# State-space stage of a three-layer model: outputs in four quarter arrays and two PSUM banks, taps in the angles' bank, skip term on TensorE, low parts on GpSimd

## The chip, the cores and the metric

The kernel runs on one core of one Trainium2 chip. The metric is device time in microseconds (us) of one execution; lower is better. The kernel before takes 1944.32 us, the median of three runs (1943.21, 1944.32, 1945.85).

## What is computed

Three layers on 512 tokens of width 1024, in float32: a state-space (S5) mixer with a gated output projection and a feed-forward block, an attention layer with selected keys and its feed-forward block, and a hybrid layer with its feed-forward block. The change lies in the first mixer alone. Cut to that:

```python
def s5_mixer(u, lam_re, lam_im, log_dt, b_re, b_im, c_re, c_im, d_skip, w_glu):
    lam = lax.complex(lam_re.astype(f32), lam_im.astype(f32))
    dt = jnp.exp(log_dt.astype(f32))[:, None]
    a_bar = jnp.exp(lam * dt)                               # 64 groups x 64 states
    b_bar = ((a_bar - 1.0) / lam)[..., None] * lax.complex(b_re.astype(f32), b_im.astype(f32))
    bu = jnp.einsum('blgh,gph->blgp', ug, b_bar)            # 16 channels in a group
    _, states = lax.associative_scan(_ssm_combine, (a_seq, bu), axis=1)
    y = jnp.einsum('blgp,ghp->blgh', states, c).real.reshape(bsz, length, D_MODEL)
    y = y + d_skip.astype(f32) * u.astype(f32)
    y = jax.nn.gelu(y).astype(u.dtype)
    val, gate = jnp.split(y @ w_glu, 2, axis=-1)
    return val * jax.nn.sigmoid(gate)
```

## The kernel before

The program is written for each engine apart, with semaphores between the engines; each engine runs its own list in order. After the S5 stage come eleven phases of weight streaming ("glu", "gu0", "down0" and so on), each a long row of matrix products on TensorE (PE). Their weights come in units of 128 x 1024 numbers: SyncE (SP) issues the load of a unit, ScalarE (ACT) writes its high part (`split_hi`, L221), GpSimd (POOL) its low part (`split_lo`, L228), and PE multiplies three times (L238 to L240). Such products start when the low parts of the first two units are there.

The S5 stage works on 8 groups of channels at a time, in 8 steps e = 0 to 7: `begin` (step 0), `step` (1 to 6) and `finish` (7), each engine having its own version. The sequence is cut into 64 chunks of 8 tokens. Buffers that end in `[p]` exist twice, for even and odd steps.

- VectorE (DVE), `matrices(e)` L652: rounds the angles (L659, from PSUM), builds the input matrices `winT` from two tables and two copies of B (L665, L670, L675: 128 x 1024, both inputs in SBUF), and clamps the exact angles (L678). `recurrence(e)` L691: rotates, scans (L711) and rotates back the chunk states, L703 to L721, the sources in PSUM. `tables(e)` L723 adds the skip term `dI` to the taps `conv` (L726). `low(e)` L684 writes the low part of a finished output row (L688). A middle step is `matrices(e + 1)`, `recurrence(e)`, `tables(e + 1)`, `low(e - 1)`.
- PE, middle step: `angle_parts(e + 1)` (L842 to L844), `turn_outputs(e - 1)` (L854, 32 records), `matrices(e + 1)`: four transposes (L771), the taps (L779, 8 products in 16 records of 128 x 32), four transposes (L771); then `outputs(e)`: the products with the taps' shifted table `toep` (L810), `inputs(e + 1)` (L794), `angle_sums(e + 2)` (L836), and the 32 products of states and output tables (L820, 64 records: each float32 product is two records). `outputs` writes one PSUM bank, Y_BANK. The groups 0 to 3 have their states in partitions 0 to 63 and write there, the groups 4 to 7 use partitions 64 to 127, and the order `SIDES` alternates between the two.
- ACT, middle step: `gelu(e - 1)` (table load, L493, high part L496), `matrices_out(e + 1)` (`win` L504 twice, taps L509), `angles(e + 1)` (table load, L473 to L478), `outputs(e)` (L516, the outputs out of PSUM), the decays (L481) and the inputs (L488).
- POOL, middle step: `weigh(e + 2)` (L408), `inputs(e + 1)` (L384), `states_out(e)`: the four output tables (L392, 128 x 512 each), after a wait for the outputs of step e - 2.
- SP: eight DMAs in a step (L338) shift the taps into `toep`; when those of step 7 have been issued, it waits for the last matrices, output tables and decays, whose buffers the weights take over, and issues the first loads of "glu" (L201).

The waits that the order hangs on, in SP's `shift_taps` and in DVE's `tables`:

```python
                sp.wait_ge(S["conv_ready"], e + 1)
                sp.wait_ge(S["y_done"], e + 1)
```

```python
                dve.wait_ge(S["conv_copied"], e + 2)
                dve.tensor_tensor(conv[0:GH, :, :], conv[0:GH, :, :], dI[0:GH, bass.ds(e * QG, QG), :], ALU.add)
                dve.drain().then_inc(S["conv_ready"], 1)
```

Of the kernel before, what the change touches and what calls it, by code (L numbers as in the profile page):

```python
# [14 lines left out]
P = 128  # L15
D = 1024
# [109 lines left out]
def build(nc, d, out):  # L126

    ctx = ExitStack()
    with ctx:
# [148 lines left out]
        def s5two(name, shape):  # L278
# [31 lines left out]
            "wout_ready", "winT_ready", "psT_ready", "psT_free", "convps", "conv_copied", "conv_ready", "w_ready",  # L310
# [42 lines left out]
        PT_BANK, ANG_BANK, CONV_BANK, Z_BANK, Y_BANK, YT_BANK = (0, 4), 1, 2, (3, 6), 5, 7  # L353
# [7 lines left out]
        round_ps, exact_ps = (ps[:, ANG_BANK, n * QP * NC:(n + 1) * QP * NC] for n in range(2))  # L361
        b_raw = [braw[:, n, :].rearrange("p (g h) -> p g h", h=GH) for n in range(2)]

        def s5_gpsimd(pool):
# [31 lines left out]
            def skips():  # L396

                pool.wait_ge(S["par_landed"], 16)
                pool.wait_ge(S["cx_landed"], 16 * 3)
                pool.tensor_tensor(dskip[0:GH, :], dskip[0:GH, :], gain5[0:GH, :], ALU.mult)  # L400
                pool.drain()
                pool.tensor_tensor(dI[0:GH, :, :], bc(dskip[0:GH, :], 2, GH), bc(ident[0:GH, 0:GH], 1, G), ALU.mult)
# [31 lines left out]
        def s5_scalar(act):  # L434
# [63 lines left out]
            def matrices_out(e, p, use):  # L498
# [8 lines left out]
                if not (isinstance(before, int) and before == 0):  # L507
                    act.wait_ge(toep_landed[1 - p], before * (16 * CH))
                act.activation(conv[:].rearrange("p (q g) h -> p q g h", q=2),  # L509
                               ps[:, CONV_BANK, 0:QG * GH].rearrange("p (g q h) -> p q g h", g=QP, q=2), ACT.Copy)\  # L510
                    .then_inc(S["conv_copied"], 1)

            def outputs(e):
                act.wait_ge(S["yT_ready"], e + 1)
                act.wait_ge(S["y_done"], e + 3)
                act.activation(y_q[:].rearrange("p t (g h) -> p g t h", g=4),  # L516
                               ps[:, Y_BANK, :].rearrange("p (g t h) -> p g t h", g=4, t=CH), ACT.Copy)\
                    .then_inc(S["y_evac"], 1)

            def begin(e, p, use):  # L520
# [5 lines left out]
                act.activation(t8T[0:2 * QP, 4:6, :], ps[0:2 * QP, Y_BANK, 0:2 * P].rearrange("p (e n) -> p e n", n=P), ACT.Copy)\  # L526
# [22 lines left out]
        def s5_vector(dve):  # L549
# [102 lines left out]
            def matrices(e, p):  # L652
# [5 lines left out]
                if on_pe:  # L658
                    dve.tensor_scalar(whole[:], round_ps, ROUND, -ROUND, ALU.add, ALU.add).then_inc(S["ang_rounded"], 1)  # L659
                else:  # L660
                    dve.tensor_scalar(turns, ang_sum[:], ROUND, -ROUND, ALU.add, ALU.add)
# [14 lines left out]
                if on_pe:  # L676
                    dve.wait_ge(S["ang_exact"], e)
                    dve.tensor_scalar(ang[:].rearrange("p g c -> p (g c)"), exact_ps, 0.5, -0.5, ALU.min, ALU.max)\  # L678
# [4 lines left out]

            def low(e, p):  # L684

                dve.wait_ge(S["yhi_ready"], e + 1)
                at_ = bass.ds(e, 1)
                dve.tensor_tensor(h_lo[:, at_, :], t32[p][:].unsqueeze(1), h_hi[:, at_, :].bitcast(F32), ALU.subtract)\  # L688
                    .then_inc(S["ylo_ready"], 1)
# [33 lines left out]
            def tables(e, p):  # L723

                dve.wait_ge(S["conv_copied"], e + 2)
                dve.tensor_tensor(conv[0:GH, :, :], conv[0:GH, :, :], dI[0:GH, bass.ds(e * QG, QG), :], ALU.add)  # L726
                dve.drain().then_inc(S["conv_ready"], 1)

            def begin(e, p, use):
# [4 lines left out]
                tables(e, p)  # L734
# [3 lines left out]
                tables(e + 1, 1 - p)  # L738

            def step(e, p, use):  # L740
                matrices(e + 1, 1 - p)
                recurrence(e, p)
                tables(e + 1, 1 - p)
# [10 lines left out]
        def s5_tensor(pe):  # L754
# [10 lines left out]
            def matrices(e):  # L765
# [9 lines left out]
                turned(0)  # L775
                pe.wait_ge(S["conv_copied"], e + 1)
                for g in range(QP):
                    for r in range(2):
                        conv_last = pe.matmul(ps[:, CONV_BANK, 2 * g * GH:2 * (g + 1) * GH],  # L779
                                              winT[:, QP * r + g, :, :].rearrange("p t h -> p (t h)"),  # L780
                                              c_pair[:, bass.ds(e * QP + (GP * r + g), 1), :].rearrange("p a h -> p (a h)"),
                                              start=r == 0, stop=r == 1)
# [16 lines left out]
            SIDES = [g + 4 * half for g in range(4) for half in range(2)]  # L799

            def outputs(e, p, use, between=None):
# [4 lines left out]
                def out_of(g):  # L806
                    return ps[half_of(g), Y_BANK, (g % 4) * P:(g % 4 + 1) * P]

                for g in SIDES:
                    pe.matmul(out_of(g), u_q[p][:, g, :], toep[p][:, :, g, :], start=g % 4 == 0, stop=False)  # L810
# [5 lines left out]
                for r in range(2):  # L816
                    for table in (wout[p], wout_im[p]):
                        for g in SIDES:
                            rows, v = half_of(g), QP * r + g % QP
                            last = pe.matmul(out_of(g), zout[p][rows, v, :], table[rows, v, :, :], start=False,  # L820
                                             stop=r == 1 and table is wout_im[p] and g % 4 == 3)
                last.then_inc(S["y_done"], 1)

            def transposed_ratio():

                pe.wait_ge(S["turn"], 3)
                for e in range(2, NQ):
                    bank = YT_BANK if e < 6 else Y_BANK
# [4 lines left out]
            def angle_sums(e):  # L833

                pe.wait_ge(S["ang_reduced"], e)
                pe.matmul(round_ps, t8T[0:2 * QP, e - 2, :], chunks[0:2 * QP, 0, :], start=True, stop=True)\  # L836
                    .then_inc(S["ang_ready"], 1)

            def angle_parts(e):

                pe.wait_ge(S["ang_rounded"], e - 1)
                pe.matmul(exact_ps, ident, whole[:], start=True, stop=False)  # L842
                pe.matmul(exact_ps, t8T[0:2 * QP, e - 2, :], chunks[0:2 * QP, 1, :], start=False, stop=False)
                pe.matmul(exact_ps, t8T[0:2 * QP, e - 2, :], chunks[0:2 * QP, 2, :], start=False, stop=True)\  # L844
# [1851 lines left out]
```

## Time and profile before

| | |
|---|---|
| median of three runs | 1944.32 us |
| the profiled execution, its own time | 1944.47 us |
| its span in the profile | 1942.4 us |
| of it, the S5 stage up to the first weight product | 133.56 us |
| PE busy in the span | 1890.6 us (97%) |
| DVE, ACT, POOL busy in the span | 774.6, 807.5, 856.8 us |

The profile's times count from the start of the span. "Busy" of PE counts records that overlap once. A row of a timeline gives start, length, engine, line, operation and what it writes and reads; in square brackets stands how long the engine had been idle and what ended that.

### The profile page before, as it was taken

The page shows a single profiled execution, that of the slowest core. Times are in us where ns is not written, and L with a number is a line of the kernel's source. Part 1 is how long each engine was busy: PE and PEld are TensorE (multiplying, and loading weights), DVE is VectorE, ACT ScalarE, POOL GpSimd, SP SyncE. Part 2 cuts the span into 40 slices and gives each one's busy share as a digit, 9 for nine tenths or more (in the row PEclk, how much of TensorE's full clock was granted, in tenths as well). Part 3 has the DMA queues.
Part 4 walks back from the last instruction along what each step waited for, and adds up shares of the span by engine and source line. Part 5 has one row for each costly group of instructions (what it writes and reads, how often), then busy time and mean ns, then how long its engine had stood idle before and what let it go on. Part 6 is the DMA issues. An engine that isn't in the chain of part 4 may idle for free.

```text
span 1942.4 us, 26536 instructions
## 1 busy us (share of the span) xinstructions
PE 1890.6 (97%) x9610; PEld 1528.6 (79%) x9610; DVE 774.6 (40%) x1382; ACT 807.5 (42%) x1179; POOL 856.8 (44%) x421
## 2 busy tenths in 40 slices
PE   6999999999999999999999999999998999999997
PEld 4878788888887786578888888877885888888886
DVE  7852232222016999825222200456477062222103
ACT  4663344443125444835344421446246254344211
POOL 6544354444433243844444444434335444444441
PEclk9999999999999999999999999999999999999998
DMA  2143242333232232022323232332320323323331
GB/s 107 27 148 98 74 127 87 98 96 99 96 97 87 66 98 76 1 67 89 105 86 105 90 103 95 101 98 76 131 76 1 98 90 94 104 90 98 98 97 44
DMA packets 51832, 170.81 MB, mean 88 GB/s; under 512 B 6696, under 2 KB 11560, under 8 KB 51248
## 3 DMA queue, kind: packets, MB, share of 16 engines
q1 hardware_dynamic: 50320, 164.99, 27.4%
q10 hardware_dynamic: 1440, 4.83, 0.7%
q8 instruction: 48, 0.79, 0.2%
q14 instruction: 24, 0.20, 0.0%
HBM read 165.34 MB, written 2.10 MB: 86 GB/s over the span
## 4 chain that ended last, share of the span: by engine, by line
PE 91%; DVE 5%; ACT 1%; DMA 1%; DVEq 1%; issue 1%; SPq 0%; ACTq 0%
PE ps L238 24%; PE ps L240 24%; PE ps L239 24%; PE ps L1590 3%; PE ps L1592 3%; PE ps L1591 3%; PE ps L1289 2%; PE ps L1303 1%; PE ps L1311 1%; PE ps L820 1%; DVE h_lo L1212 1%; DVE xT L1135 1%; DMA s_gains<-in_s_gain 1%; PE ps L1629 1%; PE ps L1609 0%
## 5 line engine op out<-in xcount | busy, mean ns | idle before, releaser
L228 POOL TENSOR_TENSOR w_lo<-raw,w_hi 128x1024 fp32r<-128x1024 f32 x296 | 712.8, 2417 | 972.9 <-ACT w_hi L221 972.9
L238 PE MATMUL ps<-h_hi,w_hi 128*128 128x512 f32 (+1 forms) x1456 | 570.6, 392 | 4.2 <-DVE h_lo L1212 2.8
L240 PE MATMUL ps<-h_hi,w_lo 128*128 128x512 f32 (+1 forms) x1456 | 566.8, 389 | 0.0
L239 PE MATMUL ps<-h_lo,w_hi 128*128 128x512 f32 (+1 forms) x1456 | 566.6, 389 | 0.0
L221 ACT ACTIVATE w_hi<-raw 128x1024 fp32r<-128x1024 f32 x296 | 311.5, 1057 | 487.5 <-PE ps L240 436.8
L238 PEld LDWEIGHTS ps<-h_hi,w_hi 128*128 128x128 f32 (+1 forms) x1456 | 272.2, 187 | 64.5 <-issue 7.5
L240 PEld LDWEIGHTS ps<-h_hi,w_lo 128*128 128x128 f32 (+1 forms) x1456 | 272.1, 187 | 58.3
L239 PEld LDWEIGHTS ps<-h_lo,w_hi 128*128 128x128 f32 (+1 forms) x1456 | 272.3, 187 | 57.7 <-issue 0.5
L238 PE MATMUL ps<-hid_hi,w_hi 128*128 (+1 forms) x528 | 205.4, 389 | 0.0
L239 PE MATMUL ps<-hid_lo,w_hi 128*128 (+1 forms) x528 | 205.4, 389 | 0.0
L240 PE MATMUL ps<-hid_hi,w_lo 128*128 (+1 forms) x528 | 205.4, 389 | 0.0
L1135 DVE TENSOR_TENSOR xT<-xT,ps 128x512 f32<-128x512 f32 x40 | 27.5, 688 | 391.1 <-PE ps L240 390.5
L957 ACT ACTIVATE hid_hi<-t 128x512 f32 x66 | 41.7, 632 | 297.2 <-DVE t L971 297.2
L968 DVE TENSOR_TENSOR t<-ps,spread 128x512 f32<-128x512 f32 x66 | 45.6, 691 | 285.4 <-PE ps L240 285.4
L238 PEld LDWEIGHTS ps<-hid_hi,w_hi 128*128 128x128 f32 x528 | 99.1, 188 | 20.7
L239 PEld LDWEIGHTS ps<-hid_lo,w_hi 128*128 128x128 f32 x528 | 99.1, 188 | 20.5
L240 PEld LDWEIGHTS ps<-hid_hi,w_lo 128*128 128x128 f32 x528 | 99.1, 188 | 20.5
L1590 PE MATMUL ps<-w_hi,h_hi 128*128 128x512 f32 x288 | 113.6, 395 | 1.4 <-ACT tot L2211 1.0
L1592 PE MATMUL ps<-w_hi,h_lo 128*128 128x512 f32 x288 | 112.2, 390 | 0.0
L1591 PE MATMUL ps<-w_lo,h_hi 128*128 128x512 f32 x288 | 112.1, 389 | 0.0
L966 DVE TENSOR_TENSOR sq<-ps,spread 128x512 f32<-128x512 f32 x66 | 45.6, 691 | 131.5 <-PE ps L240 130.7
L1423 POOL TENSOR_SCALAR pr<-pr,den 128x512 f32<-128x512 f32 (+2 forms) x54 | 66.2, 1247 | 25.5 <-DVE den L1451 25.5
(379 smaller groups left out, 2096.2 us busy)
## 6 DMA issues: line engine op xcount, KB each, us to landing
raw<-in_w_gu SPq DMA_DIRECT2D x132, 512.0 KB, 3.5
raw<-in_w_down SPq DMA_DIRECT2D x66, 512.0 KB, 3.5
raw<-in_w_mix SPq DMA_DIRECT2D x33, 512.0 KB, 3.5
raw<-in_w_dsa SPq DMA_DIRECT2D x29, 512.0 KB, 3.5
raw<-in_w_glu SPq DMA_DIRECT2D x16, 512.0 KB, 3.8
raw<-in_w_out SPq DMA_DIRECT2D x12, 512.0 KB, 3.5
raw<-in_w_o SPq DMA_DIRECT2D x8, 512.0 KB, 3.5
s_x<-in_xs SPq DMA_DIRECT2D x1, 2048.0 KB, 11.2
```

Of the source, the lines that this page charges most:

```text
L221: act.activation(w_hi[slot][:], raw[slot][:], ACT.Copy).then_inc(hi_ready, 1)
L228: pool.tensor_tensor(w_lo[slot][:], raw[slot][:], w_hi[slot][:].bitcast(F32), ALU.subtract)\
L238: pe.matmul(o, wh, ah, start=start, stop=False)
L239: pe.matmul(o, wh, al, start=False, stop=False)
L240: return pe.matmul(o, wl, ah, start=False, stop=stop)
L966: dve.tensor_tensor(sq[jj][:], ps[:, 2 * jj, :], spread[:], ALU.mult).then_inc(ph.scaled, 1)
L968: dve.tensor_tensor(t32[jj][:], ps[:, 2 * jj + 1, :], spread[:], ALU.mult)
L1135: dve.tensor_tensor(xT[:, o, :], xT[:, o, :], ps[:, o, :], ALU.add).then_inc(ph.x_ready, 1)
L1423: pool.tensor_scalar(p, p, a.den[:, n:n + 1], None, ALU.mult).then_inc(a.scaled, 1)
L1590: pe.matmul(o, h_hi[:, kt, toks], wh, start=(kt == 0), stop=False)
L1591: pe.matmul(o, h_hi[:, kt, toks], wl, start=False, stop=False)
L1592: last = pe.matmul(o, h_lo[:, kt, toks], wh, start=False, stop=(kt == KT - 1))
```

## The change

1. The 32 output products of a step, and the 8 products with `toep`, are spread over four quarters: the half of the partitions that the states come from gives the bank (5 or 2), and two groups of each half write partitions 0 to 63, the other two 64 to 127. The order is 0, 2, 4, 6, 1, 3, 5, 7. The outputs leave PSUM in two ACT instructions in place of one, and the rows of `w_glu` are permuted on the host's side of the layout to match.
2. The bank that the taps had goes to the outputs; the taps now share a bank with the angles. Rounded and exact angles use the same columns, and new waits keep them apart: the taps' products wait for the clamped angles (`ang_reduced`), `angle_sums` waits for the copied taps (`conv_copied`), and so does `matrices` on DVE in steps 0 and 1.
3. The skip term is one more PE product (16 rows, 128 columns) that adds into the taps. `tables` on DVE goes, and SP waits for ACT's copy.
4. `low(e - 1)` moves from DVE to POOL for six of eight steps, to the end of POOL's step.

```diff
@@ s5_sync
-                sp.wait_ge(S["conv_ready"], e + 1)
+                sp.wait_ge(S["conv_copied"], e + 2)
@@ banks
-        PT_BANK, ANG_BANK, CONV_BANK, Z_BANK, Y_BANK, YT_BANK = (0, 4), 1, 2, (3, 6), 5, 7
+        PT_BANK, ANG_BANK, Z_BANK, Y_BANKS, YT_BANK = (0, 4), 1, (3, 6), (5, 2), 7
-        round_ps, exact_ps = (ps[:, ANG_BANK, n * QP * NC:(n + 1) * QP * NC] for n in range(2))
+        angles_ps, taps_ps = ps[:, ANG_BANK, 0:QP * NC], ps[:, ANG_BANK, QP * NC:QP * NC + QG * GH]
+        def low(engine, e, p):
+            engine.wait_ge(S["yhi_ready"], e + 1)
+            at_ = bass.ds(e, 1)
+            engine.tensor_tensor(h_lo[:, at_, :], t32[p][:].unsqueeze(1), h_hi[:, at_, :].bitcast(F32), ALU.subtract)\
+                .then_inc(S["ylo_ready"], 1)
@@ s5_gpsimd, step
                 inputs(e + 1)
                 states_out(e, p)
+                low(pool, e - 1, 1 - p)
@@ s5_scalar, outputs
-                act.activation(y_q[:].rearrange("p t (g h) -> p g t h", g=4),
-                               ps[:, Y_BANK, :].rearrange("p (g t h) -> p g t h", g=4, t=CH), ACT.Copy)\
-                    .then_inc(S["y_evac"], 1)
+                for half in range(2):
+                    mine = slice(2 * half, 2 * half + 2)
+                    last = act.activation(y_q[:].rearrange("p t (g h) -> p g t h", g=4)[:, mine],
+                                          ps[:, Y_BANKS[half], :].rearrange("p (g t h) -> p g t h", g=4, t=CH)[:, mine], ACT.Copy)
+                last.then_inc(S["y_evac"], 1)
@@ s5_vector
                 matrices(e + 1, 1 - p)
                 recurrence(e, p)
-                tables(e + 1, 1 - p)
-                low(e - 1, 1 - p)
             def finish(e, p, use):
+                dve.drain()
                 recurrence(e, p)
                 dve.drain().then_inc(Gated.pair_done, 2)
-                low(e - 1, 1 - p)
-                low(e, p)
+                dve.wait_ge(S["ylo_ready"], NQ)
+                low(dve, e - 1, 1 - p)
+                low(dve, e, p)
@@ s5_tensor, matrices
                 turned(0)
+                pe.wait_ge(S["ang_reduced"], e + 1)
                 pe.wait_ge(S["conv_copied"], e + 1)
...
+                pe.wait_ge(S["skips_ready"], 1)
+                conv_last = pe.matmul(taps_ps.rearrange("p (g q h) -> p g q h", g=QP, q=2),
+                                      ident[0:GH, :],
+                                      dI[0:GH, bass.ds(e * QG, QG), :].rearrange("p (q g) h -> p g q h", q=2), start=False, stop=True)
@@ s5_tensor, outputs
-            SIDES = [g + 4 * half for g in range(4) for half in range(2)]
+            QUADRANTS = [0, 2, 4, 6, 1, 3, 5, 7]
                 def out_of(g):
-                    return ps[half_of(g), Y_BANK, (g % 4) * P:(g % 4 + 1) * P]
+                    side, half = (g % 4) // 2, g // 4
+                    at_ = (2 * half + g % 2) * P
+                    return ps[NC * side:NC * (side + 1), Y_BANKS[half], at_:at_ + P]
@@ s5_tensor, angle_sums
                 pe.wait_ge(S["ang_reduced"], e)
+                pe.wait_ge(S["conv_copied"], e + 1)
```

Where the instructions stand. On POOL, from step 1 to step 2; L408 is `weigh`, L384 `inputs`, L392 the four output tables. Before:

```order
L408 TENSOR_TENSOR s_b<-s_b,s_gains 128x2x128
L384 TENSOR_TENSOR s_x<-s_x,s_rstd_131 128x512
L392 TENSOR_TENSOR s_wout_101<-s_pw_88,s_c 128x512
L392 TENSOR_TENSOR s_wout_101<-s_pw_90,s_c 128x512
L392 TENSOR_TENSOR s_wout_im_103<-s_pw_91,s_c 128x512 x2
```

Now (the same operations have the lines L416, L391 and L399):

```order
L416 TENSOR_TENSOR s_b<-s_b,s_gains 128x2x128
L391 TENSOR_TENSOR s_x<-s_x,s_rstd_131 128x512
L399 TENSOR_TENSOR s_wout_101<-s_pw_88,s_c 128x512
L399 TENSOR_TENSOR s_wout_101<-s_pw_90,s_c 128x512
L399 TENSOR_TENSOR s_wout_im_103<-s_pw_91,s_c 128x512 x2
L368 TENSOR_TENSOR h_lo<-t_71,h_hi 128x512
```

Behind the last row the next step's `weigh`, `inputs` and output tables follow, so these now stand behind a wait for ACT's high part.

On DVE, from the end of one `recurrence` to the end of the next `matrices`. Before:

```order
L721 TENSOR_TENSOR s_zout_122<-ps,s_ztmp 128x8x63
L726 TENSOR_TENSOR s_conv<-s_conv,s_dI 16x128
L688 TENSOR_TENSOR h_lo<-t_71,h_hi 128x512
L659 TENSOR_SCALAR s_whole<-ps 128x256
L665 TENSOR_TENSOR s_winT<-s_table_81,s_b 128x1024
L670 TENSOR_TENSOR s_wtmp<-s_table_82,s_b 128x1024
L675 TENSOR_TENSOR s_winT<-s_winT,s_wtmp 128x1024
L678 TENSOR_SCALAR s_ang_1_107<-ps 128x256
```

Now:

```order
L726 TENSOR_TENSOR s_zout_122<-ps,s_ztmp 128x8x63
L670 TENSOR_SCALAR s_whole<-ps 128x256
L677 TENSOR_TENSOR s_winT<-s_table_81,s_b 128x1024
L682 TENSOR_TENSOR s_wtmp<-s_table_82,s_b 128x1024
L687 TENSOR_TENSOR s_winT<-s_winT,s_wtmp 128x1024
L690 TENSOR_SCALAR s_ang_1_107<-ps 128x256
```

Two instructions are gone between the states and the next rounding.

## Rows read from the trace of the kernel before

**Rows 1.** The page: busy time by engine, share of the span.
```profile
PE 1890.6 (97%) x9610; PEld 1528.6 (79%) x9610; DVE 774.6 (40%) x1382; ACT 807.5 (42%) x1179; POOL 856.8 (44%) x421
```

**Rows 2.** PE's timeline, one middle step (start us, us, engine, line, operation).
```profile
73.27 0.70 PE L842 MATMUL ps<-s_whole,cst 128*128 128x256 f32 x2
...
76.03 0.66 PE L771 MATMUL ps<-cst,s_winT 128*128 128x128 f32 x4
76.52 1.87 PE L779 MATMUL ps<-s_c_pair,s_winT 128*128 128x32 f32 x16
...
78.79 1.09 PE L810 MATMUL ps<-s_toep,s_u 128*64 128x128 f32 x16
79.72 1.10 PE L794 MATMUL ps<-s_x,s_win 128*64 128x64 f32 x32
80.75 0.69 PE L836 MATMUL ps<-s_chunks,s_t8T 8*128 8x256 f32 x2
81.49 1.09 PE L820 MATMUL ps<-s_wout,s_zout 64*64 64x128 f32 x16
...
85.13 0.70 PE L842 MATMUL ps<-s_whole,cst 128*128 128x256 f32 x2
```

**Rows 3.** PE's timeline, attention: two row halves, same partitions, two banks.
```profile
758.68 1.77 PE L1289 MATMUL ps<-kT,qT 64*128 64x512 f32 x8
```

**Rows 4.** DVE's timeline, one middle step.
```profile
81.26 0.27 DVE L726 TENSOR_TENSOR s_conv<-s_conv,s_dI 16x128 f32<-16x128 f32 x1
...
82.26 0.42 DVE L659 TENSOR_SCALAR s_whole<-ps 128x256 f32<-128x256 f32 x1
...
85.18 1.23 DVE L675 TENSOR_TENSOR s_winT<-s_winT,s_wtmp 128x1024 f32<-128x1024 f32 x1
86.92 0.42 DVE L678 TENSOR_SCALAR s_ang<-ps 128x256 f32<-128x256 f32 x1 [0.52 <-PE ps L844]
...
92.52 0.68 DVE L721 TENSOR_TENSOR s_zout<-ps,s_ztmp 128x504 f32<-128x504 f32 x1
```

**Rows 5.** Timelines of POOL and DVE where both run at once.
```profile
44.83 0.42 DVE L659 TENSOR_SCALAR s_whole<-ps 128x256 f32<-128x256 f32 x1
...
46.62 2.13 DVE L670 TENSOR_TENSOR s_wtmp<-s_table,s_b 128x1024 f32<-128x1024 f32 x1
47.63 2.09 POOL L392 TENSOR_TENSOR s_wout<-s_pw,s_c 128x512 f32<-128x512 f32 x1
48.83 1.97 DVE L675 TENSOR_TENSOR s_winT<-s_winT,s_wtmp 128x1024 f32<-128x1024 f32 x1
```

**Rows 6.** Timelines of POOL and ACT, middle steps.
```profile
88.41 2.17 POOL L392 TENSOR_TENSOR s_wout_im<-s_pw,s_c 128x512 f32<-128x512 f32 x2
90.76 1.28 POOL L384 TENSOR_TENSOR s_x<-s_x,s_rstd 128x512 f32<-128x512 f32 x1 [0.18 <-issue]
85.30 0.60 ACT L516 ACTIVATE s_y<-ps 128x512 f32<-128x512 f32 x1 [2.63 <-PE ps L820]
89.43 0.63 ACT L496 ACTIVATE h_hi<-t 128x512 fp32r<-128x512 f32 x1
```

**Rows 7.** A window (length, PE busy, granted clock), and PE's timeline in it.
```profile
53.50:56.90 3.40, 3.40 (x46) 0.50 0.00 0
53.69 1.97 PE L810 MATMUL ps<-s_toep,s_u 128*64 128x128 f32 x16
57.15 0.69 PE L836 MATMUL ps<-s_chunks,s_t8T 8*128 8x256 f32 x2
```

**Rows 8.** Timelines of ACT, SP and PE, the end of the stage.
```profile
114.97 0.27 ACT L509 ACTIVATE s_conv<-ps 128x128 f32<-128x128 f32 x1
117.15 6.35 SPq L338 DMA_DIRECT2D s_toep<-s_conv  x8
123.68 0.93 SPq L201 DMA_DIRECT2D raw<-in_w_glu  x2
133.56 0.47 PE L238 MATMUL ps<-h_hi,w_hi 128*128 128x512 f32 x1 [0.41 <-issue]
```

More of the change, by code:

```diff
@@ L509, in matrices_out @@
                 act.activation(conv[:].rearrange("p (q g) h -> p q g h", q=2),
-                               ps[:, CONV_BANK, 0:QG * GH].rearrange("p (g q h) -> p q g h", g=QP, q=2), ACT.Copy)\
+                               taps_ps.rearrange("p (g q h) -> p q g h", g=QP, q=2), ACT.Copy)\
                     .then_inc(S["conv_copied"], 1)
@@ L525, in begin @@
                 act.activation(t8T[0:2 * QP, 0:4, :], ps[0:2 * QP, YT_BANK, :].rearrange("p (e n) -> p e n", n=P), ACT.Copy)
-                act.activation(t8T[0:2 * QP, 4:6, :], ps[0:2 * QP, Y_BANK, 0:2 * P].rearrange("p (e n) -> p e n", n=P), ACT.Copy)\
+                act.activation(t8T[0:2 * QP, 4:6, :], ps[0:2 * QP, Y_BANKS[0], 0:2 * P].rearrange("p (e n) -> p e n", n=P), ACT.Copy)\
                     .then_inc(S["std"], 1)
@@ L778, in matrices @@
                     for r in range(2):
[L779 to L782, printed above, removed]
+                        pe.matmul(taps_ps[:, 2 * g * GH:2 * (g + 1) * GH],
+                                  winT[:, QP * r + g, :, :].rearrange("p t h -> p (t h)"),
+                                  c_pair[:, bass.ds(e * QP + (GP * r + g), 1), :].rearrange("p a h -> p (a h)"),
+                                  start=g == 0 and r == 0, stop=False)
+                pe.wait_ge(S["skips_ready"], 1)
+                conv_last = pe.matmul(taps_ps.rearrange("p (g q h) -> p g q h", g=QP, q=2),
+                                      ident[0:GH, :],
+                                      dI[0:GH, bass.ds(e * QG, QG), :].rearrange("p (q g) h -> p g q h", q=2), start=False, stop=True)
                 conv_last.then_inc(S["convps"], 1)
@@ L806, in out_of @@
                 def out_of(g):
-                    return ps[half_of(g), Y_BANK, (g % 4) * P:(g % 4 + 1) * P]
-                for g in SIDES:
-                    pe.matmul(out_of(g), u_q[p][:, g, :], toep[p][:, :, g, :], start=g % 4 == 0, stop=False)
+                    side, half = (g % 4) // 2, g // 4
+                    at_ = (2 * half + g % 2) * P
+                    return ps[NC * side:NC * (side + 1), Y_BANKS[half], at_:at_ + P]
+                for g in QUADRANTS:
+                    pe.matmul(out_of(g), u_q[p][:, g, :], toep[p][:, :, g, :], start=g % 2 == 0, stop=False)
                 if between:
@@ L817, in outputs @@
                     for table in (wout[p], wout_im[p]):
-                        for g in SIDES:
+                        for g in QUADRANTS:
                             rows, v = half_of(g), QP * r + g % QP
                             last = pe.matmul(out_of(g), zout[p][rows, v, :], table[rows, v, :, :], start=False,
-                                             stop=r == 1 and table is wout_im[p] and g % 4 == 3)
+                                             stop=r == 1 and table is wout_im[p] and g % 2 == 1)
                 last.then_inc(S["y_done"], 1)
@@ L827, in transposed_ratio @@
                 for e in range(2, NQ):
-                    bank = YT_BANK if e < 6 else Y_BANK
+                    bank = YT_BANK if e < 6 else Y_BANKS[0]
                     last = pe.transpose(ps[0:2 * QP, bank, (e - 2) % 4 * P:((e - 2) % 4 + 1) * P],
@@ L835, in angle_sums @@
                 pe.wait_ge(S["ang_reduced"], e)
-                pe.matmul(round_ps, t8T[0:2 * QP, e - 2, :], chunks[0:2 * QP, 0, :], start=True, stop=True)\
+                pe.wait_ge(S["conv_copied"], e + 1)
+                pe.matmul(angles_ps, t8T[0:2 * QP, e - 2, :], chunks[0:2 * QP, 0, :], start=True, stop=True)\
                     .then_inc(S["ang_ready"], 1)
@@ L841, in angle_parts @@
                 pe.wait_ge(S["ang_rounded"], e - 1)
[L842 to L844 removed]
+                pe.matmul(angles_ps, ident, whole[:], start=True, stop=False)
+                pe.matmul(angles_ps, t8T[0:2 * QP, e - 2, :], chunks[0:2 * QP, 1, :], start=False, stop=False)
+                pe.matmul(angles_ps, t8T[0:2 * QP, e - 2, :], chunks[0:2 * QP, 2, :], start=False, stop=True)\
                     .then_inc(S["ang_exact"], 1)
```

23 lines of the change are left out of this document (7 added, 16 removed).

## The prediction

> **What bounds the kernel now.** First the page: PE is busy 97% of the span, but only because the weight phases keep it so; the change touches none of them [rows 1]. So I read the first 133.56 us apart, until the first weight product [rows 8]. PE's timeline of a middle step shows no gap: from L842 at 73.27 to L842 at 85.13 a step takes 11.86, of which L820 has 3.64 [rows 2]. DVE's timeline shows the runner-up: its only wait is 0.52 ahead of L678, for PE's L844, so its own loop is 11.3 [rows 4]. ACT idles 2.63 before L516 in each step [rows 6]. Last, the chain at the stage's end goes by neither: taps copied by ACT at 114.97, eight DMA issues of SP from 117.15 (6.35), the first weight load at 123.68, the first product at 133.56 [rows 8]. Whatever brings that load forward counts in full, as PE is the bound from there on.
>
> **PE's part.** L820 runs 64 records in 3.50, 55 ns each: two tiles at a time, one in each half of the partitions. L794 shows that PE can pass more: 32 records in 1.03 (79.72 to 80.75), about 30 ns each with preparation, for half as many columns [rows 2]. Four tiles of 109 ns records would come to 27. I take 29, near L794's, so 1.87 for 64 and a step shorter by 1.6; the ends are 33 ns (1.4) and 27 (1.8). That both halves can write the same partitions at once, in two banks, no S5 row shows; the attention does so: eight records of 512 and 384 columns end in 1.77, where one after another would need 4 x 0.43 + 4 x 0.32 = 3.0 [rows 3]. L810 keeps two tiles at a time; I leave it.
>
> The skip term adds a product of two 128-column records. By L779, 107 ns a record, it costs 0.22; by the L836 block, also few rows, 0.74 with the changes of tile shape before and after it. I take 0.3, since it is preceded and followed by products of full width. The Trainium skill (TensorEngine Tiling (Array Packing), Key Properties) says that a change of tiling mode drains the engine. By that rule, if 16 rows are such a mode, the product would cost about 0.6, which moves the case of a bound PE below by 1.7 us and the forecast hardly. PE's step becomes 11.86 - 1.6 + 0.3 = 10.55.
>
> The new waits on PE I cost at nothing. The taps wait for L678, which ends 0.4 behind L675, while the four transposes between take 0.49 [rows 2, 4]. `angle_sums` waits for the copied taps: L810 and L794 take 1.96 from the last transpose, ACT's `win` and taps copies 1.1. ACT's second half of L516 adds about 0.15, under its idle 2.63 less the 1.6 that L820 gives up.
>
> **DVE's and POOL's part.** DVE loses L726 and L688: L659 follows 1.00 earlier [rows 4]. With the wait gone too, its own loop is 11.86 - 0.52 - 1.00 = 10.3. So without anything else PE would bound at 10.55.
>
> But the moved `low` sits on POOL between one step's four output tables and the next step's work, and it waits for ACT's high part. Before, POOL begins the tables when L820 ends, and works off most of them while DVE reads PSUM. Now the order is: L820 starts at X; high part done at X + 7.0 (before 90.06 - 81.49 = 8.6, less 1.6 [rows 2, 6]); `low` to X + 8.3 (1.1 to 1.3, by L392 and L384); `weigh` and `inputs` to X + 10.4; tables to X + 14.8 (4.4, twice 2.17) [rows 6]. DVE's three products of 128 x 1024 start 0.1 behind the next L820, at about X + 12.1. They meet.
>
> What meeting costs is seen at 45 to 51, where POOL and DVE both have two SBUF inputs: L670 takes 2.13 and L675 1.97 in place of 1.23, L392 2.09 in place of 1.09; each seems to start its work when the other's ends (L670 ends at 48.76, L392 1.0 later at 49.72, L675 1.1 later at 50.80) [rows 4 to 6]. So the second and third product lose 0.8 each, and the first the rest of what POOL is in, 0 to 1.0. Walked through step by step I get 1.5 to 1.9, so 1.7; ends are 0 (POOL is past) and 2.6. DVE's loop is 10.3 + 1.7 = 12.0, and DVE binds; PE's gain of 1.3 a step is lost behind it. The output tables are still in time: done at X + 14.8 plus two stalls, needed at X + 24. PE now waits some 0.9 for `winT` and 0.5 for the states in each step.
>
> **Begin and end.** In step 0, L726 goes from DVE, but PE's dummy products there aren't sooner done, and `angle_sums` comes where it came, plus 0.3 for the skip term; L659, which now waits for it alone, starts at 44.05 for 44.83. POOL then waits for the first high part, and DVE's three products, 1.8 us disturbed before, end at 44.05 + 4.15 = 48.2 for 50.80 [rows 4, 5]. PE's L820 runs from 44.0 to 46.0; with L842 to L854 behind it (76.03 - 73.27 = 2.76 [rows 2]) the transposes can start at 48.75, where before they waited for L675 until 50.86: -2.1, with the skip term -1.8. Before, the clock was granted at 0.50 (1.2 GHz) from 53.5 to 56.9, after PE had idled ahead of these transposes; L810 to L836 took 3.46, against 1.96 at full clock [rows 2, 7]. If the idle of 0.7 is gone, so are 1.5.
>
> At the end SP no longer waits for DVE's L726, only for ACT's copy: 117.15 - 114.97 - 0.3 for copy and signal = 1.85 [rows 8]. The six `low` on POOL leave the last tables done by 116, decays by 118, before SP needs them at 119. The GLU waits for POOL's low weights as before.
>
> **Sum**, against the profiled execution's 1944.47 (0.15 above the median): -1.8 at the begin, -1.5 clock, five steps at +0.14 = +0.7, -1.85 at the end: -4.45. Then what the new idle may cost. PE idles some 4 us from the last L820 to the last outputs' copy, which stands behind ACT's weight splits. I count one stretch at 0.50 over the first weight products, +1.5 by rows 7, and one more within the steps, 1.5 less 0.25 of slack. 1944.47 - 4.45 + 1.5 + 1.25 = **1942.8 us**. A measurement of this kernel can tell about 0.2%, 3.9 us: this is no change.
>
> **Rivals.**
>
> PE stays the bound (POOL and DVE miss each other, or the loser is POOL: L675 at 85.18 kept its 1.23, though POOL's tables start when L820 ends at 85.13 [rows 2, 4]). Then steps take 10.55: five times -1.3 = -6.5 in place of +0.7, with the rest as above and no new gaps in the steps: 1944.47 - 1.8 - 1.5 - 6.5 - 1.85 + 1.5 = 1934.3. Against it: the walk puts POOL's tables right under DVE's products in every step. Chance 0.14.
>
> The four quarters bring nothing: records of one product hold up the next, and a pair runs as before. PE's step is 12.16, the high part comes at X + 8.6, the collision remains, and steps take 12.3: +2.2; begin -0.2 (L820 keeps its length), clock -1.5, end -1.85, then +1.5: 1944.6. The attention's rows speak against it. The Trainium skill (TensorE: Matmul & The Clock Gate, Part 3) has matmuls start and end strictly in program order. By that rule, two records of one product on one tile would block the next, and this case would hold. Chance 0.17.
>
> Slower: the clock. PE now has an idle 0.9 before its transposes in every step, more than the 0.7 that stood before the fall at 53.5. If it falls after each of six, that is 6 x 1.25 = 7.5 in place of 1.25: 1949.0, slower by 0.24%; five such falls with the one over the first weight products end at 1947.8, so it decides only from the sixth on. Against it: falls seen in the trace are few, and PE's stretches without idle are long. Chance 0.07.
>
> **Chances.** The forecast's case has 0.62; a third of it, with no fall in the steps or a milder meeting, ends under 1940.4. So faster by over 0.2%: 0.14 + 0.18 = 0.32; slower by over 0.2%: 0.07 and 0.01 for a collision above 2.5; within it 0.60. The range, 1935.5 to 1946.8, leaves out most of the first and the last rival; it takes in collisions from 0.7 (five times -1.0) to 2.5 (+4).
>
> **What would show it.** L820's 64 records in about 2.0, not 3.6. L677, L682 and L687, the three products under their new lines, at 1.9 to 2.1 each from step 2 on, and at 1.23 in step 1; L399 near 2.1. A step of 12.0 from one L824 row to the next, PE idle before L768 <- DVE s_winT. SP's first toep issue of step 7 within 0.3 of ACT's copy. First weight product near 129, with a clock of 0.50 around it. I am wrong if DVE's products keep 1.23 (then 1934), if the L824 block keeps 3.6, or if the clock falls in most steps.

## The result

| | before | after |
|---|---|---|
| median of 14 runs each, same chips | 1944.96 us (1943.21 to 1949.37) | 1951.31 us (1946.13 to 1953.67) |
| ratio, 95% interval | | 1.003 (1.0023 to 1.0037) |
| the profiled execution | 1944.47 us | 1951.63 us |
| its span | 1942.4 us | 1949.8 us |
| first weight product | 133.56 us | 140.61 us |

The change makes the kernel slower by 0.3%, 6 us; I had said 1942.8 and a range to 1946.8. Of the 7.4 us between the two spans 7.05 lie ahead of the first weight product, in the S5 stage.

PE's timeline of the kernel after, over one step, answers to [rows 2]:

```profile
56.60 0.67 PE L824 MATMUL ps<-s_wout,s_zout 64*64 64x128 f32 x16
...
57.93 0.65 PE L824 MATMUL ps<-s_wout_im,s_zout 64*64 64x128 f32 x16
58.51 0.70 PE L847 MATMUL ps<-s_whole,cst 128*128 128x256 f32 x2
...
63.24 0.96 PE L768 MATMUL ps<-cst,s_winT 128*128 128x128 f32 x4 [1.91 <-DVE s_winT L687]
64.00 3.46 PE L777 MATMUL ps<-s_c_pair,s_winT 128*128 128x32 f32 x16
...
69.16 1.98 PE L814 MATMUL ps<-s_toep,s_u 128*64 128x128 f32 x16
...
73.83 0.67 PE L824 MATMUL ps<-s_wout,s_zout 64*64 64x128 f32 x16
```

The part that was to save time does: L824 takes 1.9 us (56.60 to 58.51), where L820 took 3.64. But then PE stands for 1.91 and waits for DVE's L687, and behind that gap everything on PE takes nearly twice as long: L777 3.46 for 1.87, L814 1.98 for 1.09. The window view says why. Its columns are window, length, busy us of PE, PEld, DVE, ACT and POOL (with counts), granted clock, DMA share and GB/s:

```profile
63.60:73.60 10.00, 10.00 (x75) 8.93 (x73) 5.31 (x9) 4.20 (x8) 7.43 (x7) 0.50 0.04 11
91.10:104.40 13.30, 13.30 (x136) 11.58 (x136) 8.26 (x12) 4.34 (x9) 7.55 (x8) 0.50 0.09 23
122.10:128.20 6.10, 6.10 (x74) 5.43 (x77) 3.86 (x7) 3.60 (x7) 3.63 (x4) 0.50 0.05 11
```

For these 29 us PE is busy without a gap, and the granted clock is 0.50 (1.2 GHz). Before, one such stretch of 3.4 us lay in the steps [rows 7]. The two timelines of DVE and POOL over the same step show where the gap comes from:

```profile
57.00 2.10 DVE L677 TENSOR_TENSOR s_winT<-s_table,s_b 128x1024 f32<-128x1024 f32 x1
59.17 1.97 DVE L682 TENSOR_TENSOR s_wtmp<-s_table,s_b 128x1024 f32<-128x1024 f32 x1
61.22 1.97 DVE L687 TENSOR_TENSOR s_winT<-s_winT,s_wtmp 128x1024 f32<-128x1024 f32 x1
...
73.94 0.42 DVE L670 TENSOR_SCALAR s_whole<-ps 128x256 f32<-128x256 f32 x1 [4.57 <-PE ps L841]
74.28 1.21 DVE L677 TENSOR_TENSOR s_winT<-s_table,s_b 128x1024 f32<-128x1024 f32 x1
```
```profile
52.70 1.26 POOL L368 TENSOR_TENSOR h_lo<-t,h_hi 128x512 fp32r<-128x512 f32 x1 [7.46 <-ACT h_hi L505]
...
55.84 2.18 POOL L399 TENSOR_TENSOR s_wout<-s_pw,s_c 128x512 f32<-128x512 f32 x2
57.98 4.13 POOL L399 TENSOR_TENSOR s_wout_im<-s_pw,s_c 128x512 f32<-128x512 f32 x2
...
68.86 2.17 POOL L399 TENSOR_TENSOR s_wout_im<-s_pw,s_c 128x512 f32<-128x512 f32 x2
```

POOL's `low` waits 7.46 for ACT's high part, and the tables behind it fall on DVE's three products: 6.04 us in place of 3.7. At half clock PE then takes so long that DVE waits 4.57 for it, POOL's tables end at 71.0, and the next three products miss them (1.21 at 74.28). So steps alternate. The first L824 rows of the eight steps stand at 46.01, 56.60, 73.83, 84.42, 100.75, 113.00, 127.09 and 134.70: steps of 10.6, 17.2, 10.6, 16.3, 12.3 and 14.1. Before, from 43.70 to 117.06, the same six took 73.4 (the first 14.1, the others 11.9 each); now they take 81.1.

The end of the stage runs much as before, only later. Timelines of ACT, SP and PE, for [rows 8]:

```profile
124.08 0.27 ACT L518 ACTIVATE s_conv<-ps 128x128 f32<-128x128 f32 x1
124.38 6.32 SPq L338 DMA_DIRECT2D s_toep<-s_conv  x8
131.02 1.76 SPq L201 DMA_DIRECT2D raw<-in_w_glu  x4
140.61 0.47 PE L238 MATMUL ps<-h_hi,w_hi 128*128 128x512 f32 x1 [0.53 <-issue]
```

### The profile page after: what moved, and what is told of

The parts are those of the page before. It is cut to its first block, busy times and chain, and to the rows that moved or that the text cites. A ratio compares the mean times of both kernels' runs of the same rounds, so it can differ in the third digit from the quotient of the medians.

```text
span 1949.8 us, 26576 instructions
## 1 busy us (share of the span) xinstructions
PE 1894.1 (97%) x9626; PEld 1529.0 (78%) x9626; DVE 770.9 (40%) x1368; ACT 808.1 (41%) x1187; POOL 863.6 (44%) x427
## 4 chain that ended last, share of the span: by engine, by line
PE 92%; DVE 4%; ACT 1%; DMA 1%; DVEq 1%; issue 1%; ACTq 0%; SPq 0%
PE ps L238 24%; PE ps L240 24%; PE ps L239 24%; PE ps L1595 3%; PE ps L1597 3%; PE ps L1596 3%; PE ps L1294 2%; PE ps L1308 1%; PE ps L1316 1%; DVE h_lo L1217 1%; DVE xT L1140 1%; PE ps L777 1%; DMA s_gains<-in_s_gain 1%; PE ps L796 1%; PE ps L1634 1%
```

## The experiments

The theory: POOL's tables meet DVE's products, the input matrices come late, PE stands, and then it runs at half clock. Every kernel below was timed beside the kernel before, whose median was 1945.05 to 1945.29: e1 to e4 on one chip, e5 to e8 on a second, the rest on a third. A trace is that of a single run of its kernel. The steps' times are from the first L824 row (or what answers to it) of each step.

**e1: everything but the moved subtraction.** In `step` of the engines:

```
 POOL:  states_out(e, p)
-       low(pool, e - 1, 1 - p)
 DVE:   recurrence(e, p)
+       low(dve, e - 1, 1 - p)
```

> The change with one part undone: the low parts are subtracted by VectorE again, behind its recurrence, as before the change; four quarters, shared bank and the skip product stay. Theory T (the subtraction on GpSimd pushes the output tables under VectorE's products of the next step, the input matrices come late, TensorE stands for 1 to 2 us before the transposes and runs at half clock for 7 to 14 us after it): GpSimd's first table starts 1.3 us earlier, meets only the third of VectorE's 128x1024 products, but VectorE's own loop is about 1.0 us longer by the subtraction, so its matrices are still late: idle before the transposes 0.3 to 1.3 us, one to three falls of the clock, 1940 to 1950 us. Rival R1 (the idle comes from L824 being 1.7 us shorter, whoever subtracts): idle of 1.5 us or more before the transposes and three or more falls of over 6 us, 1950 to 1953. Rival R2 (what is new at the taps' bank, its waits and the skip product, lengthens TensorE's own path): the time stays at 1951 within 1.

1948.33 us, ratio 1.0013 (1.0004 to 1.0022). In the profiled run (1945.09, the fastest of eleven) the steps are 12.3, 12.8, 11.4, 12.7, 11.3 and 12.1, the idle before the transposes 3.6 in six places, and three stretches at half clock lie in the steps, short ones of 3.4 us each. As the theory has it; R1's long falls didn't come, and R2 is out. It also shows how small a gap a fall may follow: at 87.28 PE had stood 0.58, the clock fell at 89.9, and the second transposes at 90.01 take 1.11 instead of 0.66.

```profile
87.28 0.66 PE L768 MATMUL ps<-cst,s_winT 128*128 128x128 f32 x4 [0.58 <-DVE s_winT L686]
...
90.01 1.11 PE L768 MATMUL ps<-cst,s_winT 128*128 128x128 f32 x4
```

**e2: the same subtraction on POOL, one step later, where it waits for nothing.**

```
 POOL:  states_out(e, p)
-       low(pool, e - 1, 1 - p)
+       if e >= 2:
+           low(pool, e - 2, p)
```

In `finish` POOL does `low(pool, e - 2, p)` behind its tables.

> The change, with GpSimd subtracting each low part one step later and behind its output tables: nothing stands before the tables but the inputs, so they start as soon as L824 ends. Work and engines are as in the change. T: tables run from about X+11.9 for 4.9 us as before, where X is the start of a step's L824, and reach only the third of VectorE's three products; VectorE's loop is near 11.2, idle before the transposes under 0.6 us, at most one fall of the clock in the steps, 1937 to 1943 us. R1 (the shorter L824 makes the idle): idle of 1.1 to 1.9 us before the transposes as in the change, 1950 to 1953. R2 (the taps' bank): 1951 within 1.

1944.21 us (1938.67 to 1948.62), ratio 0.9995 (0.9986 to 1.0004): 7 us under the change, with the same work on the same engines. The profiled run (1939.38, the second fastest of eleven) has steps of 11.0 and 11.2 behind a first one of 12.2, and no half clock from 45 to 122. POOL's and DVE's timelines of a step:

```profile
78.65 1.28 POOL L391 TENSOR_TENSOR s_x<-s_x,s_rstd 128x512 f32<-128x512 f32 x1
81.55 3.78 POOL L399 TENSOR_TENSOR s_wout<-s_pw,s_c 128x512 f32<-128x512 f32 x2 [1.62 <-PE ps L826]
```
```profile
79.56 1.44 DVE L679 TENSOR_TENSOR s_winT<-s_table,s_b 128x1024 f32<-128x1024 f32 x1
81.08 1.23 DVE L684 TENSOR_TENSOR s_wtmp<-s_table,s_b 128x1024 f32<-128x1024 f32 x1
82.38 1.97 DVE L689 TENSOR_TENSOR s_winT<-s_winT,s_wtmp 128x1024 f32<-128x1024 f32 x1
```

POOL now waits for PE's outputs, not for ACT, and only the third product is hit. R1, as the whole cause, and R2 fall: PE's blocks and the shared bank are those of the change. (That the short L824 has its part in the harm all the same, e7 shows below.) What I didn't expect is the spread. By the mean clock over the span, the two runs at 0.991 and 0.992 took 1939.38 and 1938.67, the three at 0.986 took 1944.71 to 1948.62. By their clocks, falls still came in most runs. At 1944.21 the median lies 1.2 over my range.

**e3: the change, with PE kept busy in the gap.**

```
         turn_outputs(e - 1)
+        pe.wait_ge(S["psT_free"], (e + 1) * 2 + 1)
+        for _ in range(2):
+            pe.matmul(ps[:, PT_BANK[0], :], ident, cst[:, 0:T], start=True, stop=True)
         matrices(e + 1)
```

> The change, plus two 128x512 products of constants per step on TensorE, between the transposes of the outputs and those of the matrices, that is in the idle time; they start each bank's half anew and nothing reads them. VectorE and GpSimd are untouched, so VectorE's products still take near 2.0 us. T, with the clock as what costs: the granted clock stays at 2.4 GHz through the steps, L768's wait for VectorE shrinks to under 0.6 us by the records, steps are near 12.0 as predicted, 1940 to 1944 us. If the half clock is only a symptom of TensorE being idle and costs nothing itself: the falls go and the time stays at 1950 to 1952. R1 gives the same as T here; R2 gives 1951 to 1954, since two more products lie on TensorE's path.

1946.81 us, ratio 1.0008 (0.9999 to 1.0017). Window 45 to 122 and one stretch of PE's timeline:

```profile
45.00:122.00 77.00, 75.77 (x1174) 59.51 (x1166) 65.61 (x88) 54.69 (x93) 46.06 (x39) 1.00 0.11 28
```
```profile
73.71 1.98 PE L883 MATMUL ps<-cst 128*128 128x512 f32 x4
75.53 0.60 PE L768 MATMUL ps<-cst,s_winT 128*128 128x128 f32 x4
75.97 1.87 PE L777 MATMUL ps<-s_c_pair,s_winT 128*128 128x32 f32 x16
```

The clock stays at 1.00, and the time falls by 4.5 though 12 products more are computed: the half clock is a cost of its own. From one L768 row to L824, 75.53 to 81.34, it takes 5.8; in the change, behind the gap, 10.6 (63.24 to 73.83). It is 2.8 over my range because I had sized the products wrongly: two take 2.0 us, not 0.9, and PE alone needs 12.3 a step with them (69.04 to 81.34).

**e4: L824 in another order.** `QUADRANTS = [0, 6, 1, 7, 2, 4, 3, 5]`.

> The change, with the eight groups of L824 in another order: two diagonal quarters alternate at a time, first the groups on one diagonal, then those on the other. The same products in the same number; TensorE's block becomes as long as before the change, near 3.6 us at full clock instead of 1.9. If TensorE's speed in this block were worth anything, the kernel would be slower: 1953 to 1957. T and R1 both have it faster: TensorE is busy until the matrices come, so the idle before the transposes is under 0.5 us, the clock stays up, steps are bound by TensorE at about 11.9, 1943 to 1947 us. R2: 1951 or more.

1951.3 us, ratio 1.0029 (1.0018 to 1.0041), the change's time and its falls. Its premise was false: from first to last record the block took 1.76, against 1.71 in the change. I had counted two quarters at a time, but in this order each pair is followed by the other pair. So it tests nothing about cover, and e6 and e7 were made for that.

**e5: the kernel before, with the moved subtraction alone** (as the change has it, behind POOL's tables).

> The kernel before the change, with one part of the change alone: low parts subtracted on GpSimd behind the output tables; two halves in one bank, three banks and the sum of the taps on VectorE stay. Theory T2 (after the first four runs: the harm is the step's interplay, VectorE late by the collisions, TensorE standing, then half clock): VectorE's products take 1.6 to 2.0 us as in the change, its loop is the length before less 0.7 plus 1.7, near 12.3, against TensorE's 11.86; L820 at 3.64 covers most of it, idle before the transposes 0 to 0.6 us, none or one fall more than before: 1944 to 1948 us. Rival (moving the subtraction is harmless by itself): 1945 within 0.7 and VectorE's products at 1.23. Rival (it is the whole cause): 1950 or more with three falls over 6 us.

1948.39 us, ratio 1.002 (1.001 to 1.0029), at a clock of 1.00 from 45 to 122. Steps of 12.4 to 13.5 after one of 11.9: DVE binds even against the old, long L820. Its timeline over a step:

```profile
84.52 1.97 DVE L678 TENSOR_TENSOR s_wtmp<-s_table,s_b 128x1024 f32<-128x1024 f32 x1
86.56 1.97 DVE L683 TENSOR_TENSOR s_winT<-s_winT,s_wtmp 128x1024 f32<-128x1024 f32 x1
...
94.64 1.24 DVE L727 TENSOR_TENSOR s_conv<-s_conv,s_dI 16x128 f32<-16x128 f32 x1
```

L727, the sum of the taps that took 0.27 as L726 [rows 4], takes 1.24 under POOL's tables. The time is 0.4 over my range, and the loss comes without any half clock in the steps. The move isn't harmless by itself, and it isn't the whole cause either.

**e6 and e7: two halves instead of four quarters.** Both have the old `out_of(g)`, `ps[half_of(g), bank, (g % 4) * P:(g % 4 + 1) * P]`, the old order of groups and weights; e6 has a bank for each half, e7 one bank for both.

> The change with L824 as before it (even and odd products in the two diagonal quarters, each half of the groups on its own rows, the old order of the weights), but each half in a bank of its own. ScalarE copies two halves of 64 partitions. B (two banks make L824 fast, not four quarters; e4's block of two quarters at a time took 1.76 us like the change's): L824 1.7 to 1.9 us, time as the change, 1949 to 1953. Q (four quarters make it fast, and e4 owed its speed to the moments in which products of both diagonals were in flight): L824 3.4 to 3.6 us.

> The change with its first part undone whole: L824's products in two halves of one bank, one ScalarE copy of 128 partitions, the old order of the weights; shared taps' bank, skip product and GpSimd's subtraction stay. Both B and Q have L824 back at 3.4 to 3.6 us. R1, which e4 could not test since its block stayed short, and T2 agree on more cover: the idle before the transposes shrinks under 0.6 us, at most one fall over 3.4 us in the steps, steps of 12.0 to 12.4, and a slower block makes the kernel faster than the change by 3 to 7 us: 1944 to 1948. If cover is not what matters (the length of L824 simply adds to the step): 1953 to 1960.

e6: 1948.46 us, ratio 1.0017 (1.0008 to 1.0026). e7: 1947.01 us, ratio 1.0005 (0.9996 to 1.0014), within its range. The trace of e6 is of its fastest run, that of e7 of its slowest. PE's timeline of e6, one quarter of the block, and the window 47 to 122 of e7:

```profile
57.84 1.09 PE L822 MATMUL ps<-s_wout,s_zout 64*64 64x128 f32 x16
58.76 1.04 PE L822 MATMUL ps<-s_wout_im,s_zout 64*64 64x128 f32 x16
```
```profile
47.00:122.00 75.00, 73.51 (x1074) 63.49 (x1072) 67.83 (x84) 50.79 (x81) 52.46 (x38) 1.00 0.10 26
```

Two banks alone bring nothing: 3.44 from first to last record in both, so it is the four quarters (Q). And e7, with L824 twice as long, is 4.3 us faster than the change. Two of DVE's three products take 1.97 there too, but PE works on meanwhile: its waits for `winT` sum to 0.2 from 44 to 126, and the clock holds. That is the shortest statement of the result: under a late DVE, a faster PE only stands longer, and pays for standing with the half clock. (e6 is 2.9 faster, but its interval and the change's overlap.)

**e8: e2 plus one of e3's products per step.**

> e2 (low parts one step later on GpSimd) plus one of the two 128x512 products of e3 per step. T2: e2's steps of 11.0 us are VectorE's own loop and stay; TensorE's work grows from about 10.6 to 11.0 and it stands under 0.5 us per step; the falls of the clock in the steps, which came in some runs of e2 and not in its profiled one, go: median 1938 to 1941, spread of single runs under 4 us. Rival (e2's spread from 1938.7 to 1948.6 has another source): median 1943 to 1945 and the same spread.

1943.99 us (1941.26 to 1945.06), ratio 0.9991 (0.9982 to 1.0). The spread falls from 9.9 in e2, on another chip, to 3.8, as T2 had it; the median stays, as the rival had it, 3 us over T2's range. As e3 had shown, the product costs 1.0, and the steps of the profiled run are 11.4 to 11.5 long, not 11.0.

**e9, e10, e11: products of constants around the steps**, six ahead of the first `inputs` in `begin`, three ahead of the last `outputs`, two ahead of the last `turn_outputs`; in e2, in the change and in the kernel before.

> e2 (low parts one step later) plus products of constants only where TensorE stood around the steps: six 128x512 ones while the first input matrices are copied (the granted clock fell at 29.7 in every kernel so far), three while the last taps are shifted, two before the last outputs are turned (falls at 125 to 136, so that the weights' products begin at half clock). None in the steps. T2: no fall at 29.7, first L824 of the steps at 43.3 to 44.0 instead of 45.2, steps of 11.0, weight products begin at 124.5 to 126 at the full clock: 1936 to 1941 us median. If those products are in the way (they cost 0.43 each at the full clock and 0.86 at the half one): 1944 to 1948.

> The change as it is, plus the same eleven products outside the steps. Low parts before the next tables, as in the change. T2: begin and end give back 1.5 to 4 us, the steps keep their falls of 7 to 14 us of half clock: 1947 to 1950. If the begin's fall is what shifts the steps into collision (in the change every step was 0.7 us late before the first table), the steps' falls go too: 1941 to 1945.

> The kernel before the change, plus the same eleven products outside the steps. It prices the ends alone: the fall at 29.7 goes (six products L862 from 5.3 us to 2.7), the one at 125 too; TensorE is bound in the steps anyway: faster by 1.5 to 4 us, 1941 to 1943.5. If the half clock at begin and end is covered by other engines: 1945 within 0.7.

e9 1944.91 us, ratio 0.9993 (0.9984 to 1.0002); e10 1948.23, 1.002 (1.001 to 1.0029); e11 1945.03, 0.9997 (0.9989 to 1.0006). All three were planned with the wrong size of such a product, 0.43 where it takes 0.9. e9 and e11 missed T2's ranges by 3.9 and 1.5 and lie where their rivals had them. e11 shows best why: no fall is left in its trace from 20 to 160, and still it takes what the kernel before takes, since the products need the time that the full clock gives back. PE's timeline of e11:

```profile
27.62 5.32 PE L826 MATMUL ps<-cst 128*128 128x512 f32 x12
32.86 1.15 PE L794 MATMUL ps<-s_x,s_win 128*64 128x64 f32 x32
```

No fall at 29.7 any more, but L794 starts at 32.86, in the kernel before at 30.06. e9's profiled run (1945.23) lost more than that: PE stood 1.85 ahead of L770 at 52.53, and the clock fell at 53.6 for 6.8 us, in a step of 15.6. e10 came within its range, 3.0 us under the change's median on the same chip (1951.23, below), though the two intervals overlap. The gaps in its steps stayed: in the profiled run (1944.44, the fastest) PE waits 1.90, 1.13 and 1.01 ahead of the transposes, each time with a fall behind it, so the fall at the begin isn't what makes the tables meet DVE's products. Its single runs go with the clock: 1944.44 and 1945.05 at a mean of 0.991, 1953.12 and 1953.62 at 0.986.

**e12, e13, and the change once more.** e12 is e2 with two, one and three such products in the same places; e13 has also one 128x256 product per step right ahead of L824.

> e2 again plus products of constants around the steps, now of measured size: such a 128x512 product is two records and takes 0.9 us, twice what e9 and e10 were planned with, so two stand in the 2.6 us wait of the begin, one in the 1.7 us wait for the last taps, three in the 3.4 us wait for the last outputs' copy; none lies on a path by itself. T2 (e2's runs from 1938.7 at a mean clock of 0.992 to 1948.6 at 0.986 differ by falls of the clock, and some of these begin outside the steps): median 1938 to 1942 with the clock at 0.990 or more in most runs. Rival V (the spread comes from where GpSimd's tables meet VectorE's products, which those products don't change): median 1943 to 1946, and runs of 1946 or more with the clock at 0.990 or more.

> e12 plus one 128x256 product of constants (two records, 0.45 us by half of that) per step right before L824's second part, where e2 waited 0.3 to 1.0 us for VectorE's s_zout. T2: steps stay at 11.0 to 11.1, no falls in the steps, the spread of single runs under 4 us, median 1938 to 1941. V: 1943 to 1946 with the clock at 0.991 or more in all runs.

> The change itself, unaltered, beside the other two on one chip. T2: 1949 to 1953 at a mean clock of 0.982 to 0.985; any run under 1948 has its clock above 0.986. V: runs of equal clock differ by over 3 us.

| | median us | single runs | ratio to before |
|---|---|---|---|
| e12 | 1942.26 | 1939.83 to 1948.23 | 0.999 (0.9981 to 0.9999) |
| e13 | 1941.64 | 1940.57 to 1946.74 | 0.9985 (0.9976 to 0.9994) |
| the change | 1951.23 | 1948.66 to 1952.74 | 1.0029 (1.0019 to 1.004) |

e13 beats both kernels, by 0.15% and 0.5%; the first is small, but its interval leaves out 1. Of its eleven runs nine had a mean clock of 0.991 or more and took 1940.57 to 1943.78; the one at 0.988 took 1946.74. In e12 the four at 0.992 took 1940.47 to 1941.23, the three at 0.988 1945.45 to 1948.23. The medians lie 0.3 and 0.6 above T2's ranges and 0.7 and 1.4 under V's; V's runs of 1946 or more at a high clock didn't come, but e13's spread is 6.2, not under 4, by that one run. And the mean clock isn't all: e12's four runs at 0.990 took 1939.83, 1942.26, 1942.81 and 1944.52. The change's own runs all had 0.983 to 0.985.

The profiled runs say more on T2 and V. e12's (1939.83, the fastest of eleven) has a stretch at half clock of 10.2 us in the steps, from 50.9, behind a gap of 0.78. e13's (1941.64, the median) has none in the steps, but they take 10.7 to 12.9, not 11.0 to 11.1, and in the longest all three of DVE's products are hit and PE stands 1.63, with no fall behind it (DVE's and PE's timelines):

```profile
67.67 2.19 DVE L679 TENSOR_TENSOR s_winT<-s_table,s_b 128x1024 f32<-128x1024 f32 x1
69.93 2.14 DVE L684 TENSOR_TENSOR s_wtmp<-s_table,s_b 128x1024 f32<-128x1024 f32 x1
72.15 1.97 DVE L689 TENSOR_TENSOR s_winT<-s_winT,s_wtmp 128x1024 f32<-128x1024 f32 x1
```
```profile
74.17 0.66 PE L770 MATMUL ps<-cst,s_winT 128*128 128x128 f32 x4 [1.63 <-DVE s_winT L689]
```

So both have a part in the spread: falls of the clock, and where the tables meet DVE's products. Why a run of one and the same kernel has a fall and another none stays open.

## Why the prediction was wrong

**PE's part: right.** L820's records were put at 29 ns for 55; 64 take 1.71 from first to last, 27 ns, my lower end. e6 confirms that it is the quarters, and the rival that they bring nothing is out. The skip product was put at 0.3 and takes 0.41 (77.77 to 78.18 in e3, from L782's row to that of the next transposes). By the drain rule of the Trainium skill (TensorEngine Tiling (Array Packing), Key Properties) I had noted 0.6 as a case, so the trace is between the two. The new waits at the shared bank cost PE nothing: in the change's trace no row of L777 or L841, which stand behind them, has an idle time.

**DVE and POOL: right in kind and size.** The meeting was put at 1.7, with the ends 0 and 2.6. Step 2 has 2.10 + 1.97 + 1.97, which is 2.35 over 3.69, a step of e3 1.72 + 1.97 + 1.23, 1.2 over it. That step 1 and each step behind a slow one would be spared (1.21 at 74.28) I had for step 1 only.

**Begin: 1.6 too early.** I had the transposes of step 1 1.8 sooner; they start at 50.68 for 50.86, 0.2 sooner. I had the first L824 row at 44.0; it came at 46.01. L824's shorter block is there (-1.7), but PE's first L768 row was 0.7 late already (24.78 for 24.04), the dummy products took 6.41 for 5.32 (the half clock that had begun ahead of them lasted 6.8 for 3.4), and the skip product stood there with another 0.4. I had the dummy products not "sooner done"; that they could be later done I hadn't priced. The fall at 53.5 did stay away, as I said: from the transposes to the first L824 row of step 1 PE takes 5.9 for 6.9.

**Steps: the step that failed is the price of a fall**, "1.5 less 0.25 of slack", and with it the one fall that I allowed in the steps. I took the length of the one stretch in the steps of before, 3.4 us, for the length of any. The three in the steps lasted 10.2, 13.7 and 6.8. The first cost 4.8 (10.6 from L768 to L824, where e3 takes 5.8). The Trainium skill (TensorE: Matmul & The Clock Gate, HAM oscillation — how this bites in real kernels) puts the cost at half of the throttled time. By that rule the estimate is 5.1 for 10.2, and this trace agrees. So three falls did what my slower rival wanted six for: the five steps at +0.14 were to give +0.7 and the fall 1.25, and from the first L824 row of step 1 to that of step 6 they took 70.5 for 59.3, +11.2. That rival named the right mechanism, place and direction, and had a chance of 0.07 since "falls seen in the trace are few". But its own argument said that the idle would be longer than the one that had stood before the fall at 53.5, and in every step. It came in three of the six, since DVE's products miss the tables in the first step and behind each step with a long stretch at half clock; there it was 1.91, 1.14 and 1.58, and each time the clock fell. A gap of that size is no certain sign: e13 stood 1.63 and e2 1.23 (ahead of L770 at 51.21) without a fall. A condition that a forecast itself creates in each step isn't judged by how seldom it occurs before.

**End: the step itself right, its gain lost upstream.** SP's issues now follow ACT's copy by 0.3 (124.38 on 124.08), 1.9 sooner than before. But ACT's copy is at 124.08 for 114.97, since everything ahead is late. The stretch at half clock that I had over the first weight products, +1.5, lay ahead of them, at 135.1 for 3.4.

Sum by rows, up to the first weight product, with my terms beside it:

| | measured | forecast |
|---|---|---|
| transposes of step 1 | -0.2 | -1.8 |
| from there to the first L824 row of step 1 | -1.0 | -1.5 |
| from there to ACT's last copy of the taps (67.5 for 57.2) | +10.3 | +0.7 + 1.25 |
| from there to the first weight product (16.5 for 18.6) | -2.1 | -1.85 |

That is +7.05. Of the miss, 8.3 lie in the third row. What isn't shown is how the parts would add up in a kernel without any fall. One slip of my chances: a third of 0.62 is 0.21, where I put 0.18.

## What to carry to other kernels

Before an engine on the path is made faster, look at which other engine is next, and by how much; here 0.5 us of slack stood between PE and DVE, and another part of the same change was to cost DVE 1.7 and give it back 1.0. Where a gap on PE is new and can come in every step, price it also with the half clock over the whole next step, not only with the shortest stretch seen. A small side job belongs where its input has long been ready: with the same subtraction one step later the kernel was 7 us faster, and products of constants in the remaining gaps, cut to the gap's measured length, went with another 2.6 in e13. That last gain is not shown firmly: the two were timed on different chips, and their intervals against the kernel before (0.9986 to 1.0004, 0.9976 to 0.9994) overlap.

## What the runs showed of the hardware

- In the S5 stage the stretches at half clock last 3.4 to 13.7 us within one execution (the change's), and PE was busy throughout the three in the steps. The length of the gap ahead doesn't foretell it: 0.58 had 3.4 us behind it (e1), 0.78 had 10.2 (e12), 1.91 had 10.2 (the change), and 1.63 had no fall (e13).
- Products on quarters of the array: in all versions one quarter takes a record every 107 ns (3.44 us for 32 records in e6 and e7, 1.71 for 16 in the change). What counts in these versions is how many quarters have work, and e4's pairs in turn are as good as the change's order.
- Two engines with both inputs in SBUF: a DVE operation of 16x128 took 1.24 for 0.27 under POOL's tables (e5), so what is lost seems not to go by the size of the operation that is hit. The Trainium skill (SBUF — State Buffer, Who interferes with whom) says that a DVE instruction with two SBUF inputs contends with a GpSimd one that reads SBUF, and calls the hold on the shared ports an exclusive lock. e5's row fits that: the 0.97 that L727 lost is near the 1.1 that one table takes.
- A product of 128x512 with f32 operands is two records; two products in a row take 1.98 (e3's L883) at the full clock, six 5.32 (e11's L826).
